# Routed experts: weight rows dealt to the partitions in runs of eight (down: two), and transposes that read every eighth (second) column

## What is computed

```
scores = sigmoid(xt @ w_router)                      # 1032 tokens, 64 experts
eidx   = the 6 best experts of a token (of the 4 best groups)
y      = sum over the 6 of gate * swiglu(x, w_e_gu[e], w_e_down[e])
swiglu(x, w_gu, w_down):
    g, u = split(x @ w_gu)        # w_gu   (1024, 512)
    return (silu(g) * u) @ w_down # w_down (256, 1024)
```

## Time and profile before

| | |
|---|---|
| median of the 3 runs | 2939.24 us |
| the profiled execution, own time | 2946.87 us |
| its span, first to last instruction | 2945.1 us |
| PE busy in the span | 2564.5 us (87%) |
| weight loads (PEld) busy | 1470.6 us (50%) |
| mean granted clock of TensorE | 0.936 |
| bytes moved by DMA | 511.70 MB |

### The profile page before, as it was taken

How to read it: one execution, slowest core, us unless ns; L and a number is a source line. 1 busy time by engine, 2 the same in 40 slices (tenths; PEclk the granted TensorE clock), 3 DMA queues, 4 the chain that set the end, 5 groups by cost and what they waited for, 6 DMA issues and landing times. The chain is left out here.

```text
span 2945.1 us, 44078 instructions
## 1 busy us (share of the span) xinstructions
PE 2564.5 (87%) x14550; PEld 1470.6 (50%) x14550; DVE 1515.4 (51%) x3765; ACT 1103.8 (37%) x2376; POOL 373.3 (13%) x419
## 2 busy tenths in 40 slices
PE   4998996859989899895889969798999899999977
PEld 1443443538778687784566624344333333333332
DVE  1456544468878877784898664584111111111126
ACT  1223212449879578783655501221111111111110
POOL 0000001011011010101232131052000010000025
PEclk7999997969999899996999989898999999999988
DMA  8022158332145021206110084216989898897867
GB/s 326 17 83 84 36 177 290 142 105 72 54 151 207 5 104 36 86 6 175 36 34 18 9 272 128 101 36 238 398 315 396 327 346 327 321 372 274 317 249 276
DMA packets 252353, 511.70 MB, mean 174 GB/s; under 512 B 24138, under 2 KB 102156, under 8 KB 244761
## 3 DMA queue, kind: packets, MB, share of 16 engines
q1 hardware_dynamic: 196300, 311.88, 30.7%
q0 software_dynamic: 28640, 127.09, 11.7%
q10 hardware_dynamic: 27252, 70.69, 6.3%
HBM read 631.86 MB, written 86.93 MB: 244 GB/s over the span
## 5 line engine op out<-in xcount | busy, mean ns | idle before, releaser
L2906 PE MATMUL routed_ex_pG<-dispatch_exWG,routed_ex_XT 128*64 128x512 f32 x2048 | 459.9, 605 | 32.8 <-DMA dispatch_exWG<-in_w_e_gu 27.8
L2030 DVE TENSOR_REDUCE ssqc<-SQ 128x8 f32<-128x512 f32 x516 | 346.2, 683 | 127.1 <-ACT SQ L1833 113.6
L1744 PE MATMUL eK<-dWkv,LT 128*128 128x256 f32 x1032 | 318.8, 392 | 12.2 <-ACT SQ L1833 11.7
L1747 PE MATMUL eK<-WA,LT 128*128 128x272 f32 x1032 | 329.3, 401 | 0.0
L2906 PEld LDWEIGHTS routed_ex_pG<-dispatch_exWG,routed_ex_XT 128*64 128x64 f32 x2048 | 149.1, 140 | 338.1 <-issue 337.8
L1833 ACT ACTIVATE SQ<-eK 128x512 f32<-128x512 f32 x516 | 291.9, 602 | 59.1 <-PE eK L1747 43.5
L2997 DVE TENSOR_TENSOR routed_ex_sg<-routed_ex_sg,routed_ex_pG 128x256 f32<-128x256 f32 x64 | 27.0, 421 | 555.3 <-ACT routed_ex_sg L2954 555.3
L556 PE MATMUL in_pp<-ada_Win,in_hT 128*128 128x512 f32 (+1 forms) x640 | 280.9, 597 | 9.8 <-ACT in_pr L454 9.8
L2925 PE MATMUL routed_ex_pY<-routed_ex_WD,routed_ex_AT 128*64 128x512 f32 x1024 | 233.8, 598 | 0.9 <-DMA routed_ex_WD<-in_w_e_down 0.9
L1747 PEld LDWEIGHTS eK<-WA,LT 128*128 128x128 f32 x1032 | 202.1, 196 | 29.5 <-DVE numc L2029 0.2
L1744 PEld LDWEIGHTS eK<-dWkv,LT 128*128 128x128 f32 x1032 | 191.2, 197 | 48.2 <-ACT SQ L1833 16.9
(11 more groups left out here) (550 smaller groups left out, 3715.2 us busy)
## 6 DMA issues: line engine op xcount, KB each, us to landing
dispatch_exWG<-in_w_e_gu SPq DMA_DIRECT2D x256, 1024.0 KB
routed_ex_WD<-in_w_e_down SPq DMA_DIRECT2D x132, 1024.0 KB, 19.2
s_yblk<-routed_ex_Y ACTq DMA_DIRECT2D x64, 512.0 KB
ada_Win<-in_w_ada ACTq DMA_DIRECT2D x8, 2048.0 KB, 11.1
s_yblk<-zrows SPq DMA_DIRECT2D x15, 1024.0 KB
ada_Wada<-in_w_ada SPq DMA_DIRECT2D x8, 1024.0 KB, 16.2
ada_Win<-in_w_in ACTq DMA_DIRECT2D x4, 2048.0 KB, 11.5
dispatch_exWG<-in_w_e_gu SPq DMA_DIRECT2D x4, 2048.0 KB
```

The source lines that it names most:

```text
L1744: pe.matmul(pK[kn % 3][:, 512 + z:512 + z + HK], key, Wkv[:, 4:8, 0:NOPE], start=True, stop=True)
L1747: pe.matmul(pK[kn % 3][:, z:z + HK + 16], key, WA[:, pr, :], start=True, stop=True).then_inc(s_KN, 1)
L2030: dve.tensor_reduce(ssqc[cg % 2][:, n - 1 - tau, :], SQ[kn % 4].rearrange("p (h d) -> p h d", h=H), AX.X, ALU.add).then_inc(s_red, 1)
L2906: m = pe.matmul(pG[u][r, :], XT[u][:, k, r], WG[2 * u + v][:, k, :], start=(k == 0), stop=(k == KD - 1))
```

## The change

Which rows of an expert's matrix a partition holds is changed. Before, step k took rows 128k to 128k+127, so partition p held rows p, 128+p, 256+p, ...: eight separate rows of 2 KB. Now partition p holds rows 8p to 8p+7, which lie one after another in memory: one run of 16 KB in the first load of a buffer (L2518), and 8 KB in each of the two halves of the later loads. For the down weights partition p holds rows 2p and 2p+1, a run of 8 KB instead of two of 4 KB. Bytes, loads, buffers and waits stay as they are.

The tokens have to follow: step k now needs rows (columns of `X`) k, 8+k, 16+k, ..., so the transpose reads every eighth column of `routed_ex_X` (a step of 32 bytes inside a partition), and for `routed_ex_av` every second column (8 bytes), through a helper `every`. The number and sizes of the transposes are the same; so are the matmuls.

```
-  sp.dma_start(G["ex_WG"][v][:, :, :], T["w_e_gu"][0, bass.ds(expert[v], 1)].rearrange("a (k p) n -> p (a k) n", p=P))...
+  sp.dma_start(G["ex_WG"][v][:, :, :], T["w_e_gu"][0, bass.ds(expert[v], 1)].rearrange("a (p k) n -> p (a k) n", p=P))...
...
+  every = lambda t, step, k: t[:, :].rearrange("p (r k) -> p k r", k=step)[:, k, :]
...
-  rows = T["w_e_gu"][0, bass.ds(load[v] % NE, 1), 512 * m:512 * m + 512, :]
-  sp.dma_start(WG[v][:, half(m), :], rows.rearrange("a (k p) n -> p (a k) n", p=P),
+  rows = T["w_e_gu"][0, bass.ds(load[v] % NE, 1)].rearrange("a (p k) n -> p (a k) n", p=P)
+  sp.dma_start(WG[v][:, half(m), :], rows[:, half(m), :],
...
-  sp.dma_start(WD[v][:, :, :], T["w_e_down"][0, ...].rearrange("a (k p) n -> p (a k) n", p=P), ...     # both places
+  sp.dma_start(WD[v][:, :, :], T["w_e_down"][0, ...].rearrange("a (p k) n -> p (a k) n", p=P), ...
...
-  m = pe.transpose(pX[n][:, k * P:(k + 1) * P], X[b][:, (4 * n + k) * P:(4 * n + k + 1) * P], c("ident"))   # and X[u] in turn_first
+  m = pe.transpose(pX[n][:, k * P:(k + 1) * P], every(X[b], KD, 4 * n + k), c("ident"))
...
-  m = pe.transpose(pA[:, k * P:(k + 1) * P], av[u][:, k * P:(k + 1) * P], c("ident"))
+  m = pe.transpose(pA[:, k * P:(k + 1) * P], every(av[u], 2, k), c("ident"))
```

More of the change, by code:

```diff
@@ L2517, in _ @@
             for v in range(4):
-                sp.dma_start(G["ex_WG"][v][:, :, :], T["w_e_gu"][0, bass.ds(expert[v], 1)].rearrange("a (k p) n -> p (a k) n", p=P)).then_inc(G["s_wg"][v], 16)
+                sp.dma_start(G["ex_WG"][v][:, :, :], T["w_e_gu"][0, bass.ds(expert[v], 1)].rearrange("a (p k) n -> p (a k) n", p=P)).then_inc(G["s_wg"][v], 16)
         @block.scalar
@@ L2840, in weights @@
                     sp.wait_ge(s_wd0[v], 16)
-                    sp.dma_start(WD[v][:, :, :], T["w_e_down"][0, bass.ds(load[v] % NE, 1)].rearrange("a (k p) n -> p (a k) n", p=P),
+                    sp.dma_start(WD[v][:, :, :], T["w_e_down"][0, bass.ds(load[v] % NE, 1)].rearrange("a (p k) n -> p (a k) n", p=P),
                                  cond=load[v] >= NE, bounds_check="skip_entire_dma").then_inc(s_wd[v], 16)
@@ L2844, in _ @@
             for v in range(4):
-                sp.dma_start(WD[v][:, :, :], T["w_e_down"][0, bass.ds(expert[v], 1)].rearrange("a (k p) n -> p (a k) n", p=P)).then_inc(s_wd0[v], 16)
+                sp.dma_start(WD[v][:, :, :], T["w_e_down"][0, bass.ds(expert[v], 1)].rearrange("a (p k) n -> p (a k) n", p=P)).then_inc(s_wd0[v], 16)
             run(sp, weights)
@@ L2879, in turn_first @@
                     for k in range(4):
-                        m = pe.transpose(pX[n][:, k * P:(k + 1) * P], X[u][:, (4 * n + k) * P:(4 * n + k + 1) * P], c("ident"))
+                        m = pe.transpose(pX[n][:, k * P:(k + 1) * P], every(X[u], KD, 4 * n + k), c("ident"))
                     m.then_inc(s_xt, 1)
```

## The result

The change makes the kernel faster: 2922.69 us in the median of 4 runs against 2940.43 us, a ratio of 0.9936 (95% interval 0.9921 to 0.9950). Two repeats gave 0.9927 (0.9908 to 0.9947) and 0.9924 (0.9903 to 0.9944). I had forecast 2963 us, slower; the kernel became faster. The time lies inside the stated range only because that range took in both signs, and 2 us from my rival "half rate" (2925 us).

A forecast was written before the change was run, and what follows sets the result against it. Weight transfers were taken to bound the routed stage early, PE late. Token transposes +58, activation transposes +3, gathers +1, waits and clock -38 gave +24 us on 2939.2: 2963 us, slower, 8-in-10 range 2916 to 2975.

The forecast's parts named there:

- half rate: Rival: the strided stationary load loses only a factor of two and stays behind its matmul; -14 us, 2925 us; 0.27 (or free).
- What bounds the kernel: Routed stage: early part follows weight transfers, late part is PE's alone; faster weights can give back at most 43 us.
- Transfers: Routed-stage weight loads: longer pieces cut PE's waits and the clock's price by 19 us together, bounds 0 and 43.
- the 3%: Saving in the routed stage's DMA work, some 650 us, from gate and up pieces going from 395 to 419 GB/s.
- Transposes of the tokens: 528 transposes whose stationary load steps by 32 bytes: 1.67 ns a column, +110 ns each, 58 us; bounds 0 and 72.
- Transposes of the activation: 128 transposes stepping by 8 bytes: the free-standing first load of each of 64 blocks shows 53 ns more, 3 us.
- Slack from slower transposes: Early stretch, 13 pairs: slower transposes give transfers 25 us; with faster transfers, 38 of 43 us of waits and clock go.
- The first gathers: Token gathers at the start, 4 KB rows beside longer weight pieces: 0 to 3 us more wait, 1 us taken.
- In between: Rival: stationary load at 1.25 ns a column, transposes cost 31 us, waits and clock give 31 back; 2939 us, 0.13.
- transfers without gain: Rival: weight loads no faster beside gathers and stores, PE's slack alone removes some 30 us; 2971 us, 0.08 with full price.
- weights with priority: Rival: 8 KB weight pieces gain over gathers in the queues, all waits go, transposes at half rate; 2904 us, 0.05.
- The signs that I had named: Right: transpose load about 300 ns, eight transposes 1.8 us. Wrong: 190 to 200 ns, about 1.05 us, or unchanged waits.

The follow-up runs named there:

- The weights alone: Against the kernel before, weights laid in runs of eight (two) rows, transposes still reading neighbouring columns, output not the reference's: 2915.59 us, 0.9896.
- the gate and up weights alone: The full change without its part on the down weights, which keep 4 KB pieces; activation transposes read neighbouring columns: 2920.44 us, 0.9920 of the kernel before.
- all-4-KB version: Against the changed kernel, gate and up weights in 4 KB pieces, tokens' transposes stepping by 2, down weights as before the change: 2929.99 us, 0.9953 of the kernel before.
- the transposes alone: Against the kernel before, only the transposes read every eighth (second) column, weights laid as before, output not the reference's: 2944.38 us against 2945.11, 1.0000.

## Why the prediction was wrong

- *What bounds the kernel.* Right. PE sets the late part, transfers the early one, and the waits with their clock were all there was to gain.
- *Transfers, 19 us (bounds 0 and 43).* Right in mechanism, too small in size. The weights alone shorten the stage by 27.4 us, of which 20.5 are waits. With the full change the waits up to 2345 us went from 27.6 to 13.9, where I had 8.5 off them, and the later ones from 6.0 to 1.8, where I had 5 off. The step that was too small is the 3%: in the saturated stretch the rate rose by 5.5% (400 to 422), and by 4.8% with the gate and up weights alone. Their 11.6 of 20.02 MB at my 395 and 419 GB/s would give 3.4%. Taking 413 GB/s, that of the all-4-KB version, for 4 KB pieces, the mixes come out with about 391 for 2 KB and 424 for 8 KB, an estimate: my two rates, read from stretches that were not pure, lay too close together.
- *Transposes of the tokens, 58 us (bounds 0 and 72).* This is the step that failed. I priced the stationary load with a step of 32 bytes at 1.67 ns a column, the time in which PE draws 16 bytes when contiguous: a load of 300 ns and eight transposes in 1.8 us. Measured were 193 ns, 0.82 ns a column, and 0.99 us, and the whole group became 1.3 us dearer: the load stays behind its matmul. The 1.67 ns was a bound on what the port can give and not a cost of a line; two numbers each from a line of its own took 1.74 ns together on the moving operand. VectorE's 1.83 ns an element was a fair reading of VectorE and said nothing on this load. I took a value near the bound as the likeliest, though the same rows showed the room behind the matmul.
- *Transposes of the activation, 3 us.* 4.2 us measured: the load that stands free shows, and the second one too. That it came near is luck in part, since it used the same wrong price; two numbers to 16 bytes at 1.67 ns happens to be half rate.
- *Slack from slower transposes, 38 of 43 us removed.* 26.5 us of waits and clock went, and they went by the transfers. Slack of this kind exists, as the transposes alone show (3.8 us of waits and clock for 5.5 us of work), but the price that would have made 25 us of it was wrong.
- *The first gathers, 1 us.* 1.4 us.
- *The rival "half rate", 2925 us at 0.27.* This happened, for the reason given there. That its time is only 2 us off is luck in part: its 19 us for transfers were too small, and its 5 us for the transposes came out in their sum (1.3 and 4.2 us) but were meant for the tokens' alone. *In between, transfers without gain, weights with priority:* excluded by the loads' length, by the weights alone, and by waits of 15.8 us that remain.
- *Readings.* The pace of 121 ns includes the time from the last transpose to the down matmul; from start to start it is 109, which is why the tokens' transposes cost even less than the 5 us of half rate. The idle time of PE between 2034 and 2340 us is 28.8 us, not 31. With a load of 213 ns the pace comes out at 236 ns by the formula, not 230. None of these changes the sign of the forecast.

The signs that I had named decided it: a load of 190 to 200 ns and eight transposes in about 1.05 us meant "half rate, the kernel is faster".

## What to carry to other kernels

Where a weight matrix is read while the engines are in work all the time, give each partition neighbouring rows until a piece is 8 KB, and let the stationary operand of the transposes pick the columns: its load may stream for twice as long, provided that its matmul is still the longer of the two (105 against 107 ns here; at 119 it began to show). Don't pay with the moving operand beyond a step of 2 numbers: at a step of 4, two matmuls side by side took twice the time. And where a price is read from another engine's rows, keep it as a bound and ask what the operation hides behind before giving it a chance.

## What the runs showed of the hardware

- The load of 128 float32 columns for a transpose: 141 to 150 ns for neighbours, 188 to 210 ns for steps of 2, 4 and 8 columns. Steps of 2 and 4 cost more than 8 where all eight of a group have it and the activation's transposes read neighbours (207, 208 against 189 ns; 71.8, 71.9 against 66.7 us for the 512 matmuls). Why is open.
- The moving operand of two float32 matmuls side by side: 0.84 ns a column for neighbours, 0.88 with a step of 2, 1.74 with a step of 4.
- The 16 DMA engines in full work: 400 GB/s with pieces of 2 KB (gate and up) and 4 KB (down), 413 with 4 and 4, 419 with 8 and 4, 422 with 8 and 8, gathers and stores of 4 KB rows beside them each time.
